# A hybrid decoder step with routed experts: dense stages and experts in one engine block, DRAM rows cleared later, exponentials of the gates ahead of the modulation copies

## The chip, the cores and the metric

One core of a Trainium2 chip runs the whole step. The metric is the device time of one execution in microseconds (us), as the median of several runs. All arithmetic is float32 but for a few small matmuls of zeros, ones and small integers in bfloat16.

## What is computed

One layer for 512 prompt tokens and 32 sample tokens (8 sequences of 4) with the same weights, width 1024:

```
mod = silu(c) @ w_ada + b_ada;  sh1, sc1, g1, sh2, sc2, g2 = split(mod)
h = rmsnorm(x, norm1) * (1 + sc1) + sh1
u, gate_b, gate_c, val = split(h @ w_in)               # 1024 x 2048
pool_out = (trailing means of u, windows 2/4/8/16, minus u) @ w_pool * pool_scale
conv_out = gate_b * depthwise_conv3(gate_c * val)
x = x + g1 * (concat(pool_out, conv_out) @ w_out)
h2 = rmsnorm(x, norm2) * (1 + sc2) + sh2
logits = h2 @ w_router + b_router;  top 4 of 32;  gates = softmax(of the four)
y = sum over the four experts: gate * (((u + 1) * g * sigmoid(1.702 g)) @ w_down[e] + b_down[e])
    with g = min(h2 @ w_gate[e] + b_gate[e], 7), u = clip(h2 @ w_up[e] + b_up[e], -7, 7)
x = x + g2 * y;  out = rmsnorm(x, final_norm)
```

The new states of the pooling and of the convolution (last 15 rows of u, last 2 rows of gate_c * val) are outputs too. The kernel evaluates all 32 experts, each on up to 96 rows: each expert has three matrices of 4 MB, 402 MB in all.

## The kernel before, in words

Tokens lie in 5 tiles: 4 of 128 prompt rows (PT = 4), one of the 32 sample rows (TT = 5 in all). Every engine has its own instruction stream; an operation waits for semaphores (`wait_ge`) and raises one (`then_inc`). The program has two parts, each an `nc.Block()` of its own: `block` (L335) for the dense stages and the router, `block2` (L1250) for the experts. Between them all five engines meet at a barrier (L1050), for the SBUF tensors of the first part are given back there (`part.close()`) and those of the second are laid over them. So that no DMA still reads or writes them, SyncE (SP) ends its first part with six waits (L375 to L380): for the stored rows of h2, for the stored states, for the cleared table and for the cleared rows.

**Weights.** SP issues all weight loads, 1 MB each. The dense stages take 36 of them through a ring of six slots (L343 to L346): a slot is loaded again when TensorE (PE) is done with what it held. The experts take 384 through twelve slots (`load`, L1256); the first twelve are fetched in the first part, `first` (L348), the last eight of them when the last dense slots come free. After that a pair of loads is issued for each pair of slots that `gate_up` frees (`mm_done`).

**Input projection** (`project`, L920). It has 16 column groups f of 128 columns. Group f is 32 matmuls over all 544 tokens into one of two PSUM tiles (`zt[f % 2]`), so PE may begin group f only when group f - 2 has been read out. For f = 0 to 3 (u) and f = 4 to 7 (gate_c) ScalarE (ACT) reads it out with `leave` (L566), two activations each, and raises `z_evac`; for f from 8 on VectorE (DVE) does. Groups 0 to 7 follow one another on PE without other work between them; after group 7 come the modulation matmuls of g1 (L855).

**ACT ahead of the first `leave`.** ACT issues DMAs: w_pool, w_router, b_router, norm2, 12 pieces of the expert biases (L558), and then, at L559 to L564, two that clear rows in DRAM from an SBUF tile of zeros: `expert_rows` (2176 rows of 4 KB, 8.9 MB) and `late_rows` (640 rows, 2.6 MB). Experts scatter their results into them from the third expert on; nothing before that needs them. An engine that issues a DMA goes on when the queue has taken it, not when it has landed.

**End of the first part.** For tile t: `mix` (w_out, 16 matmuls), the residual add, the norm, `transposes`, `router`; DVE's `best` picks the four experts; h2 rows go to DRAM (`store`, on SP for tiles 0 to 2, on ACT for 3 and 4). After the last tile PE computes each token's rank within its expert (L1043 to L1047) and raises `rank_done`.

**Start of the second part.** DVE: gates minus their maximum (L1595, raises `shifted`), `rank_m`, `members(0)`; PE turns members into row numbers (`row_ids`, L1758); DVE's `ids(0)` raises `id_ready`; GpSimd (POOL) gathers the rows of expert 0 with three indirect DMAs (L1310). DVE meanwhile works out the positions, waits for ACT's exponentials (`exp_done`, L1621), normalises the gates and then turns the gathered rows (`turn_rows(0)`, L1499), which is what PE's `gate_up(0)` (L1776) waits for. PE has spread the modulation g2 over rows before that: four matmuls into PSUM tile `tp` for the prompt, and, when ACT has copied them (L1414), four into the same `tp` for the samples, copied at L1416. ACT's exponentials (L1418) stand behind both copies.

POOL then gathers for expert 1 and scatters 20 slices of the table of slots; ACT loads the table, and from expert 2 on row numbers come from it. The order of the work within an engine is that in which the code is written.

## Time and profile before

| | us |
|---|---|
| median of 3 runs | 1371.39 |
| lowest and highest run | 1368.34, 1371.46 |
| the profiled execution, its own time | 1374.72 |
| its span in the trace | 1373.0 |

| engine | busy us | share of the span |
|---|---|---|
| PE matmuls | 1250.7 | 91% |
| PE weight loads | 593.1 | 43% |
| DVE | 476.9 | 35% |
| ACT | 131.0 | 10% |
| POOL | 256.1 | 19% |

The page has 493.34 MB moved by DMA, a mean of 359 GB/s over the span. The share of busy time is a mean over stages: PE is shown as busy through most of the span, but matmuls are pipelined and their ends are modelled. The dense stages end near 286 us; the barrier stands there; the experts' loop runs from about 306 to 1340 us; the rest is the final norm. Times below are from the span's start.

### The profile page before, as it was taken

The numbers are of one execution on the slowest core, as the hardware profiler recorded it, in microseconds if no ns is written. First come the engines' busy times: TensorE is split into PE (matmuls) and PEld (weight loads), VectorE is DVE, ScalarE is ACT, GpSimd is POOL, SyncE is SP. The second block draws the span as 40 slices with busy tenths as digits, with TensorE's granted clock in tenths as the row PEclk, the third lists the DMA queues.
The fourth block names the chain that finished last, engine by engine and source line by source line (L and its number), as shares of the span: only waits on it lengthen the run. The fifth ranks groups of instructions, "written<-read, shape, count | busy, mean of one in ns | idle before, by whom it ended". The sixth has DMA issues, their size and how long they took to land. (4 is left out here: it accounts for less than half of the span.)

```text
span 1373.0 us, 32053 instructions
## 1 busy us (share of the span) xinstructions
PE 1250.7 (91%) x13745; PEld 593.1 (43%) x13745; DVE 476.9 (35%) x698; ACT 131.0 (10%) x259; POOL 256.1 (19%) x317
## 2 busy tenths in 40 slices
PE   4599999859999999999999999999999999998670
PEld 2477764432444444444444444444444445444140
DVE  1031403354333344333333344333333333333366
ACT  3100001120000000010000000000000000000012
POOL 4001110016211111122211111122211111111111
PEclk9889999969999999999999999999999999999795
DMA  9965682167999999999999999999999999999944
GB/s 324 360 256 207 211 326 92 41 268 271 406 418 419 419 420 419 419 420 418 417 419 419 419 418 419 419 419 419 417 419 418 419 420 419 420 420 420 411 166 142
DMA packets 92931, 493.34 MB, mean 359 GB/s; under 512 B 15079, under 2 KB 25923, under 8 KB 43205
## 3 DMA queue, kind: packets, MB, share of 16 engines
q1 hardware_dynamic: 73650, 449.25, 80.5%
q0 software_dynamic: 12416, 20.89, 4.6%
q10 hardware_dynamic: 6835, 22.78, 4.3%
q8 instruction: 21, 0.34, 0.1%
q14 instruction: 9, 0.07, 0.0%
HBM read 470.64 MB, written 29.38 MB: 364 GB/s over the span
## 5 line engine op out<-in xcount | busy, mean ns | idle before, releaser
L1776 PE MATMUL acc<-raw_b,ht 128*32 128x512 f32 x3024 | 336.7, 600 | 12.9 <-DMA raw_b<-in_w_up 7.8
L1776 PE MATMUL acc<-raw,ht 128*32 128x512 f32 x2928 | 324.5, 599 | 10.0 <-DMA raw<-in_w_up 10.0
L1574 DVE TENSOR_TENSOR g_sb<-acc,bias_gu 128x768 f32<-128x768 f32 x32 | 30.6, 957 | 566.5 <-PE acc L1776 566.5
L1310 POOL DMA_INDIRECT rows<-h_rows,row_next x90 | 92.0, 1023 | 700.5 <-DVE row_next L1494 681.1
L1776 PEld LDWEIGHTS acc<-raw_b,ht 128*32 128x32 f32 x3024 | 103.8, 111 | 239.8 <-issue 233.9
L1776 PEld LDWEIGHTS acc<-raw,ht 128*32 128x32 f32 x2928 | 101.6, 111 | 214.4 <-issue 209.8
L1799 PE MATMUL acc<-raw_b,at 128*32 128x256 f32 x2976 | 166.5, 379 | 0.0
L1799 PE MATMUL acc<-raw,at 128*32 128x256 f32 x2976 | 166.5, 379 | 0.0
L938 PE MATMUL acc<-h_t,raw 128*128 128x288 f32 (+1 forms) x512 | 121.5, 400 | 15.6 <-ACT raw_b L571 14.4
L1799 PEld LDWEIGHTS acc<-raw_b,at 128*32 128x32 f32 x2976 | 102.9, 110 | 70.9 <-issue 18.0
L1799 PEld LDWEIGHTS acc<-raw,at 128*32 128x32 f32 x2976 | 102.9, 110 | 57.7
L938 PEld LDWEIGHTS acc<-h_t,raw 128*128 128x128 f32 x512 | 99.0, 194 | 38.0 <-issue 16.2
L1321 POOL DMA_INDIRECT expert_rows<-y_sb,y_idx x87 | 87.0, 1000 | 26.5 <-issue 26.5
L1397 ACT ACTIVATE a_sb<-g_sb 128x768 f32<-128x768 f32 x32 | 27.0, 844 | 618.7 <-DVE g_sb L1576 618.7
L1385 ACT ACTIVATE y_sb<-y_sb,table 128x256 f32<-128x256 f32 x96 | 41.8, 498 | 337.6 <-DVE y_sb L1516 337.6
L1508 DVE STREAM_TRANSPOSE at<-a_sb 128x768 f32<-128x768 f32 x31 | 49.7, 1602 | 64.9 <-PE acc L1799 64.9
L1499 DVE STREAM_TRANSPOSE ht<-rows 128x768 f32<-128x768 f32 x31 | 49.8, 1605 | 0.2
L855 PE MATMUL acc<-raw,c_act 128*32 128x256 f32 x384 | 25.1, 407 | 14.5 <-DMA raw<-in_w_ada 14.4
L1331 POOL DMA_INDIRECT late_rows<-y_sb,late_idx x9 | 16.9, 1881 | 81.7 <-ACT y_sb L1385 79.9
L1516 DVE TENSOR_TENSOR y_sb<-acc,bias_d 128x768 f32<-128x768 f32 x32 | 30.4, 950 | 4.4 <-DMA late_rows<-y_sb,late_idx 4.4
L982 PE MATMUL acc<-raw,raw_b 128*128 128x512 f32 x64 | 31.4, 647 | 0.0
L461 POOL DMA_DIRECT2D mod_rows<-mod x12 | 6.1, 506 | 134.3 <-DVE mod L654 125.2
(237 smaller groups left out, 651.1 us busy)
## 6 DMA issues: line engine op xcount, KB each, us to landing
raw<-in_w_down SPq DMA_DIRECT2D x66, 1024.0 KB, 20.8
raw_b<-in_w_gate SPq DMA_DIRECT2D x65, 1024.0 KB
raw_b<-in_w_up SPq DMA_DIRECT2D x65, 1024.0 KB, 13.6
raw<-in_w_gate SPq DMA_DIRECT2D x63, 1024.0 KB, 16.9
raw<-in_w_up SPq DMA_DIRECT2D x63, 1024.0 KB, 18.9
raw_b<-in_w_down SPq DMA_DIRECT2D x62, 1024.0 KB, 20.2
raw<-in_w_ada SPq DMA_DIRECT2D x24, 1024.0 KB, 12.0
expert_rows<-zeros ACTq DMA_DIRECT2D x1, 8704.0 KB, 30.6
```

What stands on the lines that cost most here:

```text
L938: mm = pe.matmul(zt[f % 2][:, b, 0:hi_ - lo_], w[:, j, (f % 2) * P:(f % 2 + 1) * P], h_t[:, j, lo_:hi_], start=(j == 0), stop=(j == KT - 1))
L982: mm = pe.matmul(out_[0:r, h, :], mix_t[j][:, t * P:t * P + r], w[:, j % KC, h * HALF:(h + 1) * HALF], start=(j == GR), stop=(j == GR - 1))
L1310: pool.indirect_dma_start(rows[:, b, :], None, h2_quarter, bass.IndirectOffsetOnAxis(ap=idx[:, b:b + 1], axis=0), bounds_check=Q * NTOK - ...
L1321: pool.indirect_dma_start(y_quarter, bass.IndirectOffsetOnAxis(ap=y_idx[:, b:b + 1], axis=0), y_sb[:, b, :], None, bounds_check=Q * ROWS - ...
L1385: act.activation(y_sb[:, b, :], y_sb[:, b, :], ACT.Copy, scale=gate).then_inc(y_scaled, 1)
L1397: act.activation(s_sb[:, :, :], g_sb[:, :, :], ACT.Sigmoid, scale=ALPHA).then_inc(sig_done, 1)
L1499: dve.transpose(ht_of(e)[:, :, :, :], turned(rows)).then_inc(ht_ready, 1)
L1508: dve.transpose(at_[:, :, :, :], turned(a_sb)).then_inc(at_ready, 1)
L1516: dve.tensor_tensor(y_sb[:, :, :], y, bias_d[:, :].unsqueeze(1).to_broadcast([P, SB, CW]), ALU.add)\
L1574: dve.tensor_tensor(g_sb[:, :, :], g_ps, plus(0), ALU.add).then_inc(g_read, 1)
L1776: mm = pe.matmul(gu_ps[b][q * TB:(q + 1) * TB, :].rearrange("p (m n) -> p m n", m=2), ht_of(i)[:, b, k, :], w[:, kk, :, q * CW:(q + 1) * C ...
L1799: mm = pe.matmul(out_[q * TB:(q + 1) * TB, b, :], x[:, b, k, :], w[:, kk, q * CW:(q + 1) * CW], start=(k == 0), stop=(k == KT - 1))
```

## The change

1. The two blocks become one. The barrier goes, and with it SP's six waits. In their place each engine's second part waits for what it needs itself: SP and POOL for `rank_done` and the stored h2 rows before anything else; DVE for `rank_done`, `rows_zeroed` and `table_blank` before its first write; POOL for `table_blank` before the table scatter and for `rows_zeroed` before its third step; ACT for the stored states before the second of its last fetches (`fetch(1)`, far later), whose tile `picked1` now lies where `gate_b` lay. `gate_b` and `picked1` are allocated first in their parts for that.
2. The two DMAs that clear rows are issued by ACT after the first four `leave` instead of before them.
3. ACT computes the exponentials first in its second part, and then copies g2.
4. The sample rows of g2 go to a PSUM bank of their own (`g2_s_ps`), in four pieces of 32 rows; so PE issues all eight spreading matmuls without waiting for a copy, and ACT copies once for the prompt and four times for the samples. `down(1)` waits for the copies, as its bank is the same.

```diff
-        block = part.enter_context(nc.Block())
+        block = top.enter_context(nc.Block())
...
-            sp.wait_ge(h2_stored[0], 16 * ((TT + 1) // 2))
-            sp.wait_ge(h2_stored[1], 16 * (TT // 2))
-            sp.wait_ge(state_stored, 16 * (2 + DEC_B))
-            sp.wait_ge(state_sent, 16 * (1 + DEC_T))
-            sp.wait_ge(table_blank, 16)
-            sp.wait_ge(rows_zeroed, 32)
...
+            for g in range(GR):
+                leave(g, uext[:, g, PAST:PAST + SEQ], uext_s[:, g, :, PAST:PAST + DEC_T])
+
             act.wait_ge(pool_step, POOL_STEPS)
             for dram in (y_dram, late_dram):
                 rows_ = dram.rearrange("(p r) n -> p r n", p=P)
                 act.dma_start(rows_, zeros[:, :].unsqueeze(1).to_broadcast([P, rows_.shape[1], D]))\
                     .then_inc(rows_zeroed, 16)
...
-            for g in range(GR):
-                leave(g, uext[:, g, PAST:PAST + SEQ], uext_s[:, g, :, PAST:PAST + DEC_T])
             for g in range(GR):
                 leave(GR + g, gate_c[:, g, 0:SEQ], by_seq(gate_c[:, g, SEQ:NTOK]))
...
+            g2_s_ps = psum[:, SB, 0:QW]
...
-            block2 = experts.enter_context(nc.Block())
-
-            @block2.sync
+            @block.sync
             def _(sp):
+
+                sp.wait_ge(rank_done, 1)
+                sp.wait_ge(h2_stored[0], 16 * ((TT + 1) // 2))
+                sp.wait_ge(h2_stored[1], 16 * (TT // 2))
                 sp.dma_start(fn_bc[:, :], final_norm.partition_broadcast(P)).then_inc(fn_loaded, 16)
...
-            @block2.gpsimd
+            @block.gpsimd
             def _(pool):
 
+                pool.wait_ge(rank_done, 1)
+                pool.wait_ge(h2_stored[0], 16 * ((TT + 1) // 2))
+                pool.wait_ge(h2_stored[1], 16 * (TT // 2))
                 pool.memset(rows[:, :, :], 0.0).then_inc(rows_filled, 1)
...
                 pool.wait_ge(entries_ready, 1)
+                pool.wait_ge(table_blank, 16)
...
                 step(1)
+                pool.wait_ge(rows_zeroed, 32)
                 step(2)
...
+                    if t == 1:
+                        act.wait_ge(state_stored, 16 * (2 + DEC_B))
+                        act.wait_ge(state_sent, 16 * (1 + DEC_T))
...
-                act.wait_ge(g2_spread, 1)
-                act.activation(g2_bc[:, :], flat(tp[:, :, :]), ACT.Copy).then_inc(g2_copied, 1)
-                act.wait_ge(g2_spread, 2)
-                act.activation(g2_bc_s[:, :], flat(tp[:, :, :])[0:NS, :], ACT.Copy).then_inc(g2_copied, 1)
                 act.wait_ge(shifted, 1)
                 act.activation(gates[:, :, :], gates[:, :, :], ACT.Exp).then_inc(exp_done, 1)
+                act.wait_ge(g2_spread, 2)
+                act.activation(g2_bc[:, :], flat(tp[:, :, :]), ACT.Copy).then_inc(g2_copied, 1)
+                for q in range(Q):
+                    act.activation(g2_bc_s[:, q * QW:(q + 1) * QW], g2_s_ps[q * NS:(q + 1) * NS, :], ACT.Copy)\
+                        .then_inc(g2_copied, 1)
...
+                dve.wait_ge(rank_done, 1)
+                dve.wait_ge(rows_zeroed, 32)
+                dve.wait_ge(table_blank, 16)
                 dve.tensor_tensor(gates[:, :, :], top_v[:, :, 0:TOPK], top_v[:, :, 0:1].to_broadcast([P, TT, TOPK]),
                                   ALU.subtract).then_inc(shifted, 1)
-                dve.wait_ge(rank_done, 1)
...
-                for n, (sel_, r) in enumerate(((sel_p, P), (sel_s, NS))):
-                    if n:
-                        pe.wait_ge(g2_copied, n)
-                    for q in range(Q):
-                        mm = pe.matmul(tp[0:r, q // 2, (q % 2) * QW:(q % 2 + 1) * QW], sel_[:, q, :],
-                                       mod_g2[:, :], start=True, stop=True)
-                    mm.then_inc(g2_spread, 1)
+                for q in range(Q):
+                    mm = pe.matmul(tp[:, q // 2, (q % 2) * QW:(q % 2 + 1) * QW], sel_p[:, q, :], mod_g2[:, :],
+                                   start=True, stop=True)
+                mm.then_inc(g2_spread, 1)
+                for q in range(Q):
+                    mm = pe.matmul(g2_s_ps[q * NS:(q + 1) * NS, :], sel_s[:, q, :], mod_g2[:, :], start=True, stop=True)
+                mm.then_inc(g2_spread, 1)
                 gate_up(0)
                 gate_up(1)
+                pe.wait_ge(g2_copied, 1 + Q)
                 down(1)
```

**ACT at the input projection.** The names are tiles and tensors, `raw_b` here the buffer that holds the rows of u, `gate_c` the gates of the convolution; in brackets the semaphores that an instruction waits for. Before:

```order
L558 DMA a_bc<-in_b_down 32x256 x4
L562 DMA expert_rows<-zeros 2176x1x1024 [waits pool_step]
L562 DMA late_rows<-zeros 640x1x1024
L569 ACTIVATE raw_b<-acc 128x512 [waits z_done]
L571 ACTIVATE raw_b<-acc 128x8x4
```

And now, the first group read out and the last of the four, and what follows:

```order
L553 DMA a_bc<-in_b_down 32x256 x4
L559 ACTIVATE raw_b<-acc 128x512 [waits z_done]
L561 ACTIVATE raw_b<-acc 128x8x4
...
L559 ACTIVATE raw_b<-acc 128x512 [waits z_done]
L561 ACTIVATE raw_b<-acc 128x8x4
L572 DMA expert_rows<-zeros 2176x1x1024 [waits pool_step]
L572 DMA late_rows<-zeros 640x1x1024
L559 ACTIVATE gate_c<-acc 128x512 [waits z_done]
```

The clearing moved behind the reading out of group 3 and ahead of that of group 4.

**ACT where the two parts meet.** `out<-gate_b` are the state stores. Before:

```order
L623 DMA out<-gate_b 16x512
L1050 UNCONDITIONAL_BRANCH
L1378 UNCONDITIONAL_BRANCH [waits barrier_Pool_Activation_PE_DVE_SP_release]
L1414 ACTIVATE g_bc<-acc 128x1024 [waits g2_spread]
L1416 ACTIVATE g_bc_s<-acc 32x1024 [waits g2_spread]
L1418 ACT_TABLE_LOAD
L1418 ACTIVATE gates<-gates 128x20 [waits shifted]
L1397 ACT_TABLE_LOAD
```

And now:

```order
L619 DMA out<-gate_b 16x512
L1384 UNCONDITIONAL_BRANCH
L1423 ACT_TABLE_LOAD
L1423 ACTIVATE gates<-gates 128x20 [waits shifted]
L1425 ACTIVATE g_bc<-acc 128x1024 [waits g2_spread]
L1427 ACTIVATE g_bc_s<-acc 32x256 x4
L1403 ACT_TABLE_LOAD
```

The barrier is gone, and the exponentials stand ahead of the copies.

**SP where the two parts meet.** Before:

```order
L351 DMA raw<-in_w_up 128x2048 [waits mix_done]
L1050 UNCONDITIONAL_BRANCH [waits state_sent,table_blank,state_stored,rows_zeroed,h2_stored1,h2_stored0]
L1252 UNCONDITIONAL_BRANCH [waits barrier_Pool_Activation_PE_DVE_SP_release]
L1254 DMA fn_bc<-in_final_norm 128x1024
L1260 DMA raw_b<-in_w_gate 128x2048 [waits mm_done]
```

And now:

```order
L352 DMA raw<-in_w_up 128x2048 [waits mix_done]
L1249 UNCONDITIONAL_BRANCH
L1255 DMA fn_bc<-in_final_norm 128x1024 [waits h2_stored1,h2_stored0,rank_done]
L1261 DMA raw_b<-in_w_gate 128x2048 [waits mm_done]
```

Of the six waits two are left, with `rank_done` beside them, and no other engine waits for SP there.

## Rows read from the trace of the kernel before

**Rows 1.** Busy us and counts of each engine in a stretch, granted clock, DMA share, GB/s.

```profile
400.00:1280.00 880.00, 871.46 (x10764) 371.94 (x10760) 302.89 (x397) 66.30 (x142) 175.19 (x171) 1.00 1.01 419
```

**Rows 2.** Timeline of PE, 41 to 118 us: start, duration, idle before in brackets.

```profile
41.45 14.92 PE L938 MATMUL acc<-h_t,raw 128*128 128x256 f32 x64 [1.15 <-DVE h_t L695]
70.80 47.20 PE L938 MATMUL acc<-h_t,raw 128*128 128x256 f32 x192 [14.43 <-ACT raw_b L571]
117.94 3.66 PE L855 MATMUL acc<-raw,c_act 128*32 128x256 f32 x64
```

**Rows 3.** Timeline of ACT, 53 to 89 us.

```profile
53.07 16.85 ACTq L562 DMA_DIRECT2D late_rows<-zeros  x1
69.97 0.60 ACT L569 ACTIVATE raw_b<-acc 128x512 f32<-128x512 f32 x1 [26.28 <-issue]
...
81.38 0.60 ACT L569 ACTIVATE raw_b<-acc 128x512 f32<-128x512 f32 x1 [10.14 <-PE acc L938]
...
88.71 0.60 ACT L569 ACTIVATE raw_b<-acc 128x512 f32<-128x512 f32 x1 [6.65 <-PE acc L938]
```

**Rows 4.** Stretches around the stall, columns as in the first group.

```profile
52.00:70.00 18.00, 4.37 (x19) 3.13 (x17) 0.00 (x0) 0.03 (x1) 0.00 (x0) 0.72 1.03 379
...
76.00:78.00 2.00, 2.00 (x8) 1.62 (x7) 0.00 (x0) 0.00 (x0) 0.00 (x0) 0.80 1.01 416
```

**Rows 5.** DMA issues by line: KB each, median us to landing.

```profile
late_rows<-zeros ACTq DMA_DIRECT2D x1, 2560.0 KB, 36.1
...
expert_rows<-y_sb,y_idx POOLq DMA_INDIRECT x87, 6.0
...
h_rows<-h_row ACTq DMA_DIRECT2D x1, 512.0 KB, 8.9
...
h_rows<-h_row ACTq DMA_DIRECT2D x1, 128.0 KB, 5.6
```

**Rows 6.** Waits of SP's queue at the barrier: total us, times, longest.

```profile
SPq L378 <- DMA out<-gate_b: 15.3, 1, 15.3
```

**Rows 7.** Timeline of POOL, 290 to 312 us.

```profile
290.99 0.74 POOL L1298 MEMSET rows<- 128x768 f32 x1 [21.18 <-POOLq L1050]
...
297.13 1.01 POOL L1310 DMA_INDIRECT rows<-h_rows,row_first  x1 [0.30 <-issue]
...
311.71 1.01 POOL L1310 DMA_INDIRECT rows<-h_rows,row_first  x1 [0.30 <-issue]
```

**Rows 8.** Timeline of ACT: the last store of h2.

```profile
280.60 0.31 ACTq L594 DMA_DIRECT2D h_rows<-h_row  x1
```

**Rows 9.** Timeline of DVE, 291 to 315 us.

```profile
291.03 0.18 DVE L1595 TENSOR_TENSOR gates<-top_v 128x20 f32<-128x20 f32 x1 [6.27 <-PEq L1050]
...
293.17 0.16 DVE L1488 TENSOR_TENSOR row_first<-acc,taken 128x3 uint32<-128x3 f32 x1
...
304.18 0.17 DVE L1622 TENSOR_REDUCE e_sum<-gates 128x5 f32<-128x20 f32 x1 [6.06 <-ACT gates L1418]
...
304.95 1.55 DVE L1499 STREAM_TRANSPOSE ht<-rows 128x768 f32<-128x768 f32 x1
...
314.47 1.64 DVE L1499 STREAM_TRANSPOSE y_sb<-rows 128x768 f32<-128x768 f32 x1 [6.15 <-DMA rows<-h_rows,row_first]
```

**Rows 10.** Timeline of PE, 285 to 325 us.

```profile
285.30 0.29 PE L1047 MATMUL acc<-mask_bf,ones_bf 128*128 128x32 bf16 x5
...
299.57 1.91 PE L1809 MATMUL acc<-mod_g,sel_s 128*32 128x256 f32 x8 [1.11 <-ACT g_bc L1414]
306.56 18.50 PE L1776 MATMUL acc<-raw_b,ht 128*32 128x512 f32 x144 [5.07 <-DVE ht L1499]
```

**Rows 11.** Timeline of SP's queue: the first slots that the experts' loop frees.

```profile
314.83 0.33 SPq L1260 DMA_DIRECT2D raw_b<-in_w_gate  x1
...
319.98 0.33 SPq L1260 DMA_DIRECT2D raw_b<-in_w_gate  x1
```

**Rows 12.** A stretch before and at the start of gate_up(0), columns as in the first group.

```profile
304.00:308.00 4.00, 1.44 (x8) 0.40 (x12) 3.50 (x9) 1.35 (x2) 0.00 (x0) 0.69 0.01 4
```

More of the change, by code:

```diff
@@ L137, in sb @@
             return part.enter_context(nc.sbuf_tensor(name, shape, dt))
+        gate_b = sb("gate_b", [P, GR, NTOK])
         mod = sb("mod", [P, PARTS * QW])
@@ L146, in hybrid_step @@
         h_t = sb("h_t", [P, KT, NTOK])
-        gate_b = sb("gate_b", [P, GR, NTOK])
         gate_c = sb("gate_c", [P, GR, NTOK])
@@ L558, in _ @@
                     act.dma_start(b_raw[q * E:(q + 1) * E, m, :], b[0, :, q * CW:(q + 1) * CW]).then_inc(bias_loaded, 16)
-            act.wait_ge(pool_step, POOL_STEPS)
-            for dram in (y_dram, late_dram):
-                rows_ = dram.rearrange("(p r) n -> p r n", p=P)
-                act.dma_start(rows_, zeros[:, :].unsqueeze(1).to_broadcast([P, rows_.shape[1], D]))\
-                    .then_inc(rows_zeroed, 16)
             def leave(f, dst, dst_s):
@@ L577, in _ @@
                 leave(g, uext[:, g, PAST:PAST + SEQ], uext_s[:, g, :, PAST:PAST + DEC_T])
+            act.wait_ge(pool_step, POOL_STEPS)
+            for dram in (y_dram, late_dram):
+                rows_ = dram.rearrange("(p r) n -> p r n", p=P)
+                act.dma_start(rows_, zeros[:, :].unsqueeze(1).to_broadcast([P, rows_.shape[1], D]))\
+                    .then_inc(rows_zeroed, 16)
             for g in range(GR):
@@ L1081, in sb @@
                 return experts.enter_context(nc.sbuf_tensor(name, shape, dt))
+            picked = [sb("picked1", [P, TOPK, D])]
             rows = sb("rows", [P, SB, CW])
@@ L1113, in hybrid_step @@
             fn_bc = sb("fn_bc", [P, D])
-            picked = [sb(f"picked{b}", [P, TOPK, D]) for b in range(2)]
+            picked.insert(0, sb("picked0", [P, TOPK, D]))
             made = picked[0][:, :, :].rearrange("p k d -> p (k d)")
@@ L1376, in _ @@
                 blocks(pool, body)
-            @block2.scalar
+            @block.scalar
             def _(act):
@@ L1464, in _ @@
                                    scale=1.0 / D).then_inc(fin_sqrt, 1)
-            @block2.vector
+            @block.vector
             def _(dve):
@@ L1747, in _ @@
                 finish(TT - 1)
-            @block2.tensor
+            @block.tensor
             def _(pe):
```

## The prediction

> **What bounds the kernel now.** I read the stretches first, then PE's timeline, then the two places where PE stands still.
>
> From 400 to 1280 us the DMA engines are full: share 1.01 at 419 GB/s [rows 1]. Every weight byte passes once, so the experts' loop cannot run faster than that; its end follows from when its loads begin. A load beyond the first twelve is issued when `gate_up(0)` has freed a pair of slots, first at 314.83 us and then every 5.15 us [rows 11]. A microsecond by which that first issue comes earlier is one off the end, for what follows (the loop, the last scatter, the final norm) is unchanged by the edit. So two things count: how early the dense part ends, and how long the seam between `rank_done` and `gate_up(0)` is.
>
> *Dense part.* PE runs groups 0 and 1 from 41.45 us for 14.92, then is idle for 14.43 us until 70.80, and the row names ACT's reading out of group 0 [rows 2]. ACT does it at 69.97 us; just before stands the issue of `late_rows<-zeros`, which held ACT's queue from 53.07 for 16.85 us [rows 3]. PE's wait is thus an issue stall of ACT. After it PE is slow for a while: group 2 takes 10.58 us (70.80 to 81.38), group 3 7.33 us (81.38 to 88.71) [rows 2, 3]. The granted clock was 0.5 after the idle time and 0.80 on average from 76 to 78 us [rows 4], so it was at the lower level (1.2 GHz) until about 77 us. From 118 us on PE sets the pace (idle times of a microsecond or two), and DMA is mostly not full.
>
> *Seam.* The last rank matmul ends at 285.59 us [rows 10], but DVE begins at 291.03 and POOL at 290.99, both behind the barrier [rows 7, 9]. It was SP that came last, and SP waited for the state stores, 15.3 us long [rows 6]. After that DVE is idle 6.06 us, until 304.18, for ACT's exponentials [rows 9], which stand behind two copies that wait for PE.
>
> **The change part by part.**
>
> *Clearing later, the old stall.* Without it group 2 begins when group 1 ends. ACT's last bias DMA was handed over before 53.07 us, so group 0 (done near 48.8) is read out by 54, ahead of the 56.37 at which group 2 may start. PE then needs 7.33 us for each of groups 2 to 7: 56.37 + 6 x 7.33 = 100.35, where it was 117.94 [rows 2]. That is **17.6 us**: 14.4 of waiting, 3.2 of the low clock. The weights are no limit: those for groups 2 to 7 were asked for by 41 us.
>
> *Clearing later, the new stall.* Group 3 ends at 71.03, ACT reads it out by 71.7, hands over the first DMA, and by 72.4 stands at the second, as it did at 53.07. How long it stands is not known, since its cause is not in a row. What is known: while it stood, the DMA engines moved 16.85 x 379 GB/s = 6.4 MB [rows 3, 4], of which about 1 MB was one weight chunk. If ACT is freed when as much of the zeros has gone, 5.3 MB, and one weight chunk (the slot freed by group 3) travels with it, then 6.4 MB at 419 GB/s take 15.2 us; part of the early traffic was the tail of small loads that will be gone, so I take 14.5. ACT is free at 86.9, group 4 read out at 87.6; PE wants that PSUM tile for group 6 at 56.37 + 4 x 7.33 = 85.69. New stall **1.9 us**, too short for the clock to fall. Bounds: none (gain 17.6); or the whole 16.85 us again, a stall of 4.3 us and then the clock loss of 3.2 (gain 10.1). Taken: gain **15.7 us**. The zeros themselves, 11.5 MB, are 27 us of full DMA from 72 us, done near 100. They run beside the loads for groups 8 on, wanted at 104 us and later, and that one chunk has 18 us for what takes 3 to 5. DVE's new wait for `rows_zeroed` is 170 us behind.
>
> The Trainium skill (DMA: Bandwidth & Descriptors, Issuing engines are not separate DMA queues) speaks against zeros beside weights: DMAs of all issuers end on the same 16 engines and interleave. By it the weight chunk's 2.5 us are part of ACT's hold, as counted above (15.7 gained); were the queues apart, the hold would be 12.0 us and the stall nothing (17.6 gained).
>
> *The barrier.* DVE's first instruction moves from 291.03 to about 285.7: 5.33 us. Its table of work is otherwise the same, so `row_first` is ready at 293.33 - 5.33 = 288.0 [rows 9]. POOL must have the h2 rows: issued at 280.60 [rows 8], landing 5.6 us later [rows 5], 286.2; its memset of 0.74 ends at 287, in time. The last of three gathers is issued at 297.13 - 5.33 = 291.8 [rows 7]. SP's state wait goes to ACT's `fetch(1)`, a thousand microseconds later: free.
>
> *The exponentials.* ACT ends its state stores at 285, loads its table and has the exponentials by about 287.5. DVE reaches them at 304.18 - 6.06 - 5.33 = 292.8 and does not wait. Three small operations, and at 293.4 it is ready to turn rows. Now the gather is late, not the exponentials. The eight loads of 1 MB issued from 271 on are still under way, and gathers must land among them. In quiet a gather took 314.47 - 311.71 = 2.76 us [rows 7, 9]; under full load rows of the same size scattered to DRAM landed in 6.0 us, and 512 KB of h2 in 8.9 [rows 5]. I take 6.0, the like operation at the like load: 297.8. So `turn_rows(0)` moves from 304.95 to 297.8, **7.1 us**; by the bounds 10.4 (294.56) and 4.2 (300.7). PE follows 1.61 us behind [rows 9, 10], at 299.4.
>
> *g2.* PE's eight spreading matmuls run on without the 1.11 us wait [rows 10]; nobody waits for them. They end near 295, so PE is idle 4.4 us before `gate_up(0)`. Before, it was idle from 301.48 to 306.56 and the clock fell at about 305.5 (mean 0.69 in 304 to 308 us [rows 12]), 4.0 us in. The first pair of slots then took 8.27 us (306.56 to 314.83) where the next took 5.15 [rows 10, 11]. With 4.4 us I take the fall as still happening: 0. If it does not, 3.1 us more. ACT has three more copies; it is idle then.
>
> *Sum.* 15.7 + 7.1 = 22.8 us. Profiled execution: 1374.72 - 22.8 = 1351.9. It is 3.3 us above the median of the runs, so for the median 1371.39 - 22.8 = **1348.6 us**.
>
> **The rivals.**
>
> A. *The stall moves whole.* ACT is held long enough, or by something else than the zeros' bytes, that PE loses at group 6 what it lost at group 2. For it: the cause of the 16.85 us is in no row. Against: PE has 14.7 us of groups 4 and 5 to run meanwhile, which it did not have before. Only the seam gains: 1371.4 - 7.1 = 1364.3.
>
> B. *The seam gives nothing*: the gather comes so late behind the loads that `gate_up(0)` keeps its distance from `rank_done`, or the merged block hides a wait of its own. Against: 5.33 + 6.06 us of plain waiting go. Only the dense part gains: 1355.7.
>
> C. *Slower.* ACT is held until `late_rows` has landed, 36.1 us after its issue [rows 5]: to 72.4 + 36.1 = 108.5, group 4 out at 109.2. PE then stalls 23.5 us at group 6 and 3.2 by the clock, 26.7 against 17.6 now: 9.1 lost. With the seam at its lower bound of 4.2 the kernel takes 1376.3. A hold of h costs h - 12.6 of stall and 3.2 of clock, h - 9.4 in all, against 17.6 and the seam's gain: it decides from 31.2 us (seam 4.2) or 34.1 us (seam 7.1) upward. Against it: ACT went on after 16.85 us before, far ahead of the landing. The Trainium skill (Perfetto Trace Analysis, DMA Instruction — HWDGE) has the descriptor generator freed once all descriptors are generated, which can be long before the landing; by it ACT would not wait for a landing, and C would fall away.
>
> D. *All bounds good*: no new stall, a quick gather, the clock kept: 17.6 + 10.4 + 3.1 = 31.1, so 1340.3.
>
> **How the numbers follow.** Forecast with its own bounds (gain 14.3 to 31.1, D as its end): 0.82. B 0.07, inside them. A 0.07. C 0.04. Range: 1340 to 1358, from D to the lower bounds (1357.1) and a little for the runs' own scatter; left out are A, C and what misses the bounds, not over 0.2. A measurement of this kernel can tell about 0.3%, 4.1 us, from no change. Faster than that: forecast, A and B, 0.96 less a remainder for what I have not seen, 0.94. C in its milder form is within 4.1 us of now: 0.03 the same, 0.03 slower.
>
> **What would show it.** Right: PE's L938 row of groups 2 to 7 begins right at 56 us, with a gap of 0 to 4 us near 86 whose releaser is ACT's reading into `gate_c`; ACT's `late_rows` issue is as long as before, now near 72; the g1 matmuls at 102 instead of 118. At the seam, DVE's first operation within 0.3 us of the last rank matmul, no idle time for ACT's exponentials, but 4 to 5 us for the DMA of the gathered rows; `gate_up(0)` 13.8 us after the rank matmuls (21.0 now). Each time from 400 us on the same rows, 419 GB/s. Wrong: an idle time of over 5 us on PE near 86, a weight DMA as its releaser anywhere before 180 us, or a loop that ends no earlier although it starts earlier.

## The result, and the profile after

| | before | after |
|---|---|---|
| median, us (lowest to highest, 4 runs each) | 1371.43 (1368.34 to 1373.71) | 1349.46 (1348.49 to 1350.94) |
| the profiled execution, its own time | 1374.72 | 1349.58 |
| its span | 1373.0 | 1347.7 |

The ratio is 0.984, with a 95% interval of 0.9818 to 0.9861: 22.0 us less by the medians, where 22.8 were forecast (1348.6 predicted, 1349.46 measured). Between the two profiled executions lie 25.1 us; 3.3 of them are the profiled run of before, which lies that much above its median.

From the page after: the span, the busy times of the engines and what DMA moved in all:

```profile
span 1347.7 us, 32046 instructions
PE 1244.0 (92%) x13745; PEld 593.0 (44%) x13745; DVE 477.9 (35%) x698; ACT 131.5 (10%) x262; POOL 256.3 (19%) x317
DMA packets 92931, 493.34 MB, mean 366 GB/s; under 512 B 15079, under 2 KB 25923, under 8 KB 43205
```

The bytes are those of before and so, within 1 us, are the busy times, but for PE's 6.7 us less; 3.2 of them are group 2, which no longer runs at the low clock after a stall. The rest of the gain is idle time. The middle of the experts' loop runs as in [rows 1], at 419 GB/s:

```profile
400.00:1280.00 880.00, 860.80 (x10564) 370.11 (x10556) 299.47 (x389) 64.47 (x138) 169.99 (x165) 0.99 1.02 419
```

**The input projection after.** PE's timeline, then ACT's (start, duration, in brackets the idle time before and what ended it). They answer to [rows 2] and [rows 3]:

```profile
42.24 44.25 PE L934 MATMUL acc<-h_t,raw 128*128 128x256 f32 x192 [1.15 <-DVE h_t L691]
87.22 14.90 PE L934 MATMUL acc<-h_t,raw 128*128 128x256 f32 x64 [0.73 <-ACT gate_c L561]
102.05 3.66 PE L851 MATMUL acc<-raw,c_act 128*32 128x256 f32 x64
```

```profile
71.86 0.65 ACTq L572 DMA_DIRECT2D expert_rows<-zeros  x1
72.55 13.79 ACTq L572 DMA_DIRECT2D late_rows<-zeros  x1
86.39 0.60 ACT L559 ACTIVATE gate_c<-acc 128x512 f32<-128x512 f32 x1 [13.84 <-issue]
```

PE now runs six groups on end, 192 matmuls, where it stood still for 14.43 us after two. The hold of ACT's queue has moved with the DMAs, from 53 to 72.55 us, and is shorter, 13.79 us. PE pays 0.73 us for it at group 6. The matmuls of g1 begin at 102.05 instead of 117.94.

**The seam after.** The last rank matmul and `gate_up(0)` on PE [rows 10]:

```profile
267.92 0.29 PE L1043 MATMUL acc<-mask_bf,ones_bf 128*128 128x32 bf16 x5
275.63 1.08 PE L1822 MATMUL acc<-mod_g,sel_s 128*32 128x256 f32 x8
```

DVE across it [rows 9]:

```profile
268.25 0.18 DVE L1608 TENSOR_TENSOR gates<-top_v 128x20 f32<-128x20 f32 x1 [0.86 <-PE acc L1043]
...
275.55 0.20 DVE L1636 TENSOR_TENSOR entry<-gates,e_sum 128x20 f32<-128x20 f32 x1
280.59 1.55 DVE L1509 STREAM_TRANSPOSE ht<-rows 128x768 f32<-128x768 f32 x1 [4.85 <-DMA rows<-h_rows,row_first]
```

POOL [rows 7], with the last of the three gathers, and ACT's exponentials:

```profile
268.84 0.74 POOL L1302 MEMSET rows<- 128x768 f32 x1 [16.23 <-DMA h_rows<-h_row]
...
274.36 1.01 POOL L1314 DMA_INDIRECT rows<-h_rows,row_first  x1 [0.30 <-issue]
```

```profile
267.59 1.28 ACT L1423 ACT_TABLE_LOAD   x1 [3.00 <-issue]
268.88 0.22 ACT L1423 ACTIVATE gates<-gates 128x20 f32<-128x20 f32 x1
```

DVE goes on 0.04 us after the last rank matmul (267.92 + 0.29 = 268.21) instead of 5.4 us. The exponentials are there at 269.10, long before DVE wants them. DVE is ready to turn rows at 275.75 and then waits 4.85 us for the gathered ones. PE begins `gate_up(0)` at 282.19, 13.98 us after the rank matmuls; it was 20.97. The first two pairs of slots come free, on SP's queue [rows 11], at:

```profile
289.91 0.33 SPq L1261 DMA_DIRECT2D raw_b<-in_w_gate  x1
...
295.06 0.33 SPq L1261 DMA_DIRECT2D raw_b<-in_w_gate  x1
```

That is 24.9 us earlier than 314.83, and the span is 25.3 us shorter. The gain made by 290 us is kept to the end, as the argument on the loop had it.

### The profile page after: what moved, and what is told of

The parts are those of the page before. It is cut to its first block and busy times, and to the rows that moved or that the text cites. A ratio compares the mean times of both kernels' runs of the same rounds, so it can differ in the third digit from the quotient of the medians.

```text
span 1347.7 us, 32046 instructions
## 1 busy us (share of the span) xinstructions
PE 1244.0 (92%) x13745; PEld 593.0 (44%) x13745; DVE 477.9 (35%) x698; ACT 131.5 (10%) x262; POOL 256.3 (19%) x317
## 2 busy tenths in 40 slices
DMA packets 92931, 493.34 MB, mean 366 GB/s; under 512 B 15079, under 2 KB 25923, under 8 KB 43205
## 5 line engine op out<-in xcount | busy, mean ns | idle before, releaser
L1788 PE MATMUL acc<-raw,ht 128*32 128x512 f32 x2928 | 323.8, 597 | 10.6 <-DMA raw<-in_w_up 10.6
L1811 PEld LDWEIGHTS acc<-raw_b,at 128*32 128x32 f32 x2976 | 104.1, 110 | 69.7 <-issue 17.9
L934 PE MATMUL acc<-h_t,raw 128*128 128x288 f32 (+1 forms) x512 | 118.5, 393 | 1.9 <-DVE h_t L691 1.1
L1596 DVE SCALAR_TENSOR_TENSOR a_sb<-u_sb,g_sb 128x768 f32<-128x768 f32 x32 | 30.7, 958 | 1.1
L1592 DVE TENSOR_TENSOR g_sb<-g_sb,a_sb 128x768 f32<-128x768 f32 x32 | 30.4, 951 | 0.0
## 6 DMA issues: line engine op xcount, KB each, us to landing
expert_rows<-zeros ACTq DMA_DIRECT2D x1, 8704.0 KB, 30.7
```

Of the source, the lines that this page charges most:

```text
L934: mm = pe.matmul(zt[f % 2][:, b, 0:hi_ - lo_], w[:, j, (f % 2) * P:(f % 2 + 1) * P], h_t[:, j, lo_:hi_], start=(j == 0), stop=(j == KT - 1))
L1592: dve.tensor_tensor(g_sb[:, :, :], g_sb[:, :, :], s_sb[:, :, :], ALU.mult).then_inc(glu_done, 1)
L1596: dve.scalar_tensor_tensor(out=a_sb[:, :, :], in0=u_sb[:, :, :], scalar=1.0, in1=g_sb[:, :, :], op0=ALU.add, op1=ALU.mult).then_inc(act_re ...
L1788: mm = pe.matmul(gu_ps[b][q * TB:(q + 1) * TB, :].rearrange("p (m n) -> p m n", m=2), ht_of(i)[:, b, k, :], w[:, kk, :, q * CW:(q + 1) * C ...
L1811: mm = pe.matmul(out_[q * TB:(q + 1) * TB, b, :], x[:, b, k, :], w[:, kk, q * CW:(q + 1) * CW], start=(k == 0), stop=(k == KT - 1))
```

## The experiments

Three sets of four, each set on one chip beside the kernel before. The first chip took 1370.95 us for the kernel before (median of 11), the second 1410.83 (of 9), the third 1404.18 (of 9). So each kernel is read against the kernel before of its own set; where kernels of different sets are compared, it is by these ratios or by stretches of their own traces. The result above is not recorded with a chip; its kernel before took 1371.43 us and its loop shows 419 GB/s, as on the first chip, so its traces stand below for that kind of chip. What makes the second and third chip slower became a question of its own.

### First set: the parts of the change one by one

**Clearing later alone.** The kernel before, with the two DMAs behind the first four `leave`:

```diff
-            act.wait_ge(pool_step, POOL_STEPS)
-            for dram in (y_dram, late_dram):
...
             for g in range(GR):
                 leave(g, uext[:, g, PAST:PAST + SEQ], uext_s[:, g, :, PAST:PAST + DEC_T])
+            act.wait_ge(pool_step, POOL_STEPS)
+            for dram in (y_dram, late_dram):
...
```

> Before, with only the clearing moved behind the first four readings of ACT; barrier, copies and exponentials as before. Theory (two independent gains: dense part 15.7 us, seam 7.1 us): 14.5 to 17.5 us faster than before, near 1356 us; PE's 14.4 us idle time at group 2 gone, under 2 us at group 6; the last rank matmul near 268 to 270 us; between it and gate_up(0) still 21 us, with DVE's 6 us wait for the exponentials. Rival (the stall moves whole to group 6): within 4 us of before, an idle time of over 10 us on PE near 86 us. Rival (the dense gain only shows once the barrier is gone, since DMA must catch up anyway): under 10 us faster.

Measured: 1355.84 us (1354.36 to 1360.06), ratio 0.9881 [0.9851, 0.9911]: 15.1 us less. PE's timeline:

```profile
42.78 46.94 PE L939 MATMUL acc<-h_t,raw 128*128 128x256 f32 x192 [1.15 <-DVE h_t L696]
90.50 14.90 PE L939 MATMUL acc<-h_t,raw 128*128 128x256 f32 x64 [0.78 <-ACT gate_c L566]
```

The long stall is gone and the new one is 0.78 us, without any other edit. The seam stays long: `gate_up(0)` begins 20.8 us after the last rank matmul.

**One block and exponentials first, clearing as before.**

```diff
@@ the kernel after @@
+            act.wait_ge(pool_step, POOL_STEPS)
+            for dram in (y_dram, late_dram):
...
             for g in range(GR):
                 leave(g, uext[:, g, PAST:PAST + SEQ], uext_s[:, g, :, PAST:PAST + DEC_T])
-            act.wait_ge(pool_step, POOL_STEPS)
-            for dram in (y_dram, late_dram):
...
```

> The changed kernel with the two clearing DMAs back ahead of ACT's first reading: barrier gone, exponentials first, g2 samples in their own bank. Theory: PE's 14.4 us stall at group 2 is back, and the seam (last rank matmul to gate_up(0)) is 14 us where it was 21; 6 to 8 us faster than before, near 1364.5 us. Rival (the seam's gain is eaten by the loads, which then collide with the gather): within 4 us of before.

Measured: 1363.93 us (1361.4 to 1369.31, 8 runs), ratio 0.9951 [0.9928, 0.9974]: 7.0 us less. `gate_up(0)` begins at 296.40, 14.3 us after the last rank matmul at 282.09. ACT and PE have the old stall back, 11.35 us of it instead of 14.43, since ACT was held 14.45 us and not 16.85 and the first two groups ran longer at a lower clock:

```profile
56.19 14.45 ACTq L557 DMA_DIRECT2D late_rows<-zeros  x1
```

```profile
71.52 38.69 PE L934 MATMUL acc<-h_t,raw 128*128 128x256 f32 x159 [11.35 <-ACT raw_b L566]
```

The two halves are worth 15.1 and 7.0 us alone; their sum is 22.1, and the whole change gave 22.0. The intervals of the halves are some 4 and 3 us wide to either side, so no interaction shows, and one of a few us is not excluded by the totals. The traces narrow it: the seam takes 14.3 us in this kernel and 14.0 in the change, and the new stall is 0.78 us without the merged block and 0.73 with it.

**Exponentials behind the copies again**, in the merged block (and g2 spread through the one tile `tp`):

```diff
+                act.wait_ge(g2_spread, 1)
+                act.activation(g2_bc[:, :], flat(tp[:, :, :]), ACT.Copy).then_inc(g2_copied, 1)
+                act.wait_ge(g2_spread, 2)
+                act.activation(g2_bc_s[:, :], flat(tp[:, :, :])[0:NS, :], ACT.Copy).then_inc(g2_copied, 1)
                 act.wait_ge(shifted, 1)
                 act.activation(gates[:, :, :], gates[:, :, :], ACT.Exp).then_inc(exp_done, 1)
```

> The changed kernel with the old order at g2: prompt matmuls, copy, sample matmuls into the same bank, copy, then the exponentials. Theory (the gathered rows are what DVE waits for now, they came 4.9 us after it was ready, so the exponentials have almost that much room): exponentials ready near 13.2 us after the last rank matmul, DVE turns the rows 1 to 2.5 us later than in the changed kernel, which then takes 1 to 2.5 us more, near 1351 us. Rival (the 6.06 us wait for the exponentials was the gain, the barrier hid nothing): 5 to 6 us more, near 1355 us.

Measured: 1353.93 us (1349.14 to 1356.78), ratio 0.9865 [0.9827, 0.9902]. The total can't tell this kernel from the change; the trace can. ACT, then DVE:

```profile
281.66 1.01 ACT L1425 ACTIVATE g_bc_s<-acc 32x1024 f32<-32x1024 f32 x1 [3.71 <-PE acc L1820]
282.70 1.28 ACT L1427 ACT_TABLE_LOAD   x1
283.99 0.22 ACT L1427 ACTIVATE gates<-gates 128x20 f32<-128x20 f32 x1
```

```profile
284.31 0.17 DVE L1633 TENSOR_REDUCE e_sum<-gates 128x5 f32<-128x20 f32 x1 [8.04 <-ACT gates L1427]
...
285.09 1.55 DVE L1508 STREAM_TRANSPOSE ht<-rows 128x768 f32<-128x768 f32 x1 [0.15 <-DVE entry L1635]
```

Rows are turned 15.7 us after the last rank matmul (269.41), against 12.4 in the change: in these two executions the edit is worth 3.3 us of the seam, where I had expected 1 to 2.5. The exponentials wait for both copies, and the second copy waits 3.71 us for PE's sample matmuls. These took 3.62 us here, at a granted clock of 0.50, and 1.91 us in the kernel before [rows 10], where the clock had risen. So 1.7 of the 3.3 us hang on the clock of this execution, and 1.6 are left without it, as expected. DVE waits 8.04 us for the exponentials here (6.06 before [rows 9]); with the exponentials first it waits 4.85 us for the gather instead.

**The small DMA first.** The order of the two DMAs is swapped, nothing else:

```diff
-            for dram in (y_dram, late_dram):
+            for dram in (late_dram, y_dram):
```

> The changed kernel with the two clearing DMAs in the other order: late_rows (640 rows of 4 KB) first, expert_rows (2176 rows) second. Theory G (the second DMA is held while the descriptors of the first are still being generated, and 640 fit at once): the second issue takes under 1.5 us instead of 13.8, ACT reads out group 4 in time, PE has no idle time at group 6; 0 to 1 us faster than the changed kernel. Rival L (an issue is held until enough bytes of all the zeros have gone, or its own descriptors are out): the second issue takes 10 us or more, PE stalls at group 6 as before or longer, the time is the same or up to 5 us more.

Measured: 1350.7 us (1348.78 to 1352.26), ratio 0.9845 [0.9815, 0.9876]. ACT and PE:

```profile
73.89 0.65 ACTq L572 DMA_DIRECT2D late_rows<-zeros  x1
74.57 0.66 ACTq L572 DMA_DIRECT2D expert_rows<-zeros  x1
```

```profile
42.00 61.17 PE L934 MATMUL acc<-h_t,raw 128*128 128x256 f32 x256 [1.15 <-DVE h_t L691]
```

With 2.6 MB ahead, neither issue is held: 0.65 and 0.66 us, and PE has no gap in eight groups. So the hold of 13.8 us is the second DMA's, while something of the 8.9 MB DMA ahead of it is still to be worked off. It is no landing: in the change `late_rows` was taken after 13.79 us, and `expert_rows` landed 30.7 us after its issue. The time is the change's within the scatter, as a gap of 0.73 us has to be.

### Second set: holding back loads, and clearing too late

The change still waits 4.85 us for a gather that lands beside eight weight loads. These kernels issue the last of those loads only when the gather has landed.

**Four loads held back.**

```diff
@@ SP, first part @@
-            for n in range(XSLOTS - OUT_CH, XSLOTS):
-                sp.wait_ge(*used(DENSE_CH - XSLOTS + n))
-                first(n)
@@ SP, second part, ahead of final_norm @@
+                sp.wait_ge(row_gathered, 16 * SB)
+                for n in range(XSLOTS - OUT_CH, XSLOTS):
+                    first(n)
```

> The changed kernel, but SP keeps back the last four of the twelve first expert loads (4 MB) until the rows of the first gather have landed. Theory (the gather is late because it travels among 8 MB of loads): the rows are turned 3 to 3.5 us earlier after the last rank matmul (12.4 us in the changed kernel, 9 here), the last gather landing 2.8 us after its issue instead of 6.2; but DMA is idle before it, and the 4 MB end near 19 us after the last rank matmul, so loads go on without a gap from there: 1.5 to 4 us faster than the changed kernel. Rival (a gather needs its 6 us whatever else is under way): the rows are turned as late as before, same time. Rival (the loads kept back are missed): slower than the changed kernel by 3 us or more, with a weight DMA as releaser of gate_up(0) or gate_up(1).

Measured: 1385.11 us (1377.89 to 1385.99), ratio 0.9799 [0.9767, 0.9831]. DVE's turn of the rows:

```profile
280.23 1.57 DVE L1512 STREAM_TRANSPOSE ht<-rows 128x768 f32<-128x768 f32 x1 [1.40 <-DMA rows<-h_rows,row_first]
```

It begins 8.9 us after the last rank matmul (271.30), 3.5 us sooner than in the change, and the wait is down from 4.85 to 1.40 us. So the gather was late for the loads beside it. What that is worth in total this set can't tell, since the change itself was not run in it; by the ratios the two overlap (0.984 [0.9818, 0.9861]).

**Two loads held back** (the same edit, with `XSLOTS - 2` in place of `XSLOTS - OUT_CH` for the loads that wait).

> The same with only the last two loads (2 MB) kept back. Theory: the other six are nearly through when the gathers are issued, so the rows are turned 2.5 to 3.5 us earlier than in the changed kernel, and the 2 MB are in before the first slots come free: 3 to 5 us faster than the changed kernel, so 1 to 2 us better than with four kept back. Rival (the sum of DMA work and idle time fixes the end, so order does not count): within 1.5 us of the changed kernel.

Measured: 1384.51 us (1381.48 to 1385.57, 5 runs), ratio 0.9808 [0.9786, 0.9829]; rows turned 8.9 us after the rank matmuls. Two are as good as four.

**Two loads held back and the small DMA first.**

> Two loads kept back, and late_rows cleared ahead of expert_rows. Theory: both gains add: no idle time of PE at group 6 (0.7 us) and the seam as with two kept back; 3 to 6 us faster than the changed kernel, near 1345 us. Rival (the runs' own scatter of 2 us hides it): not to be told from the run with two kept back, which is likely for 0.7 us.

Measured: 1382.7 us (1378.97 to 1384.02, 5 runs), ratio 0.9792 [0.9769, 0.9814]; rows turned 8.8 us after the rank matmuls, no gap at group 6. Against 0.984 for the change these ratios look a little better, but their intervals overlap and the chips differ. That was left to the third set.

**Clearing behind all eight `leave`.**

```diff
@@ the kernel after @@
+            for g in range(GR):
+                leave(GR + g, gate_c[:, g, 0:SEQ], by_seq(gate_c[:, g, SEQ:NTOK]))
             act.wait_ge(pool_step, POOL_STEPS)
             for dram in (y_dram, late_dram):
...
-            for g in range(GR):
-                leave(GR + g, gate_c[:, g, 0:SEQ], by_seq(gate_c[:, g, SEQ:NTOK]))
```

> The changed kernel with the two clearing DMAs behind all eight of ACT's readings, order as in the change. Theory: ACT is held 13 to 15 us again, but from 103 us, where it has nothing to do until 172 us; no idle time of PE near 86 us, 0 to 1 us faster than the changed kernel. Rival (the zeros, 27 us of DMA from 103 us, delay the weights of the projection's groups 10 on or of sh2): an idle time of PE with a weight DMA as releaser between 115 and 150 us, 2 us or more slower.

Measured: 1395.73 us (1394.33 to 1397.43), ratio 0.9887 [0.9863, 0.991], 11 to 13 us more than its three neighbours in the set. Those also hold loads back; against the change without that, 0.984 and 0.9815 in its own two sets, it is some 7 to 10 us. The rival of the expectation came true. ACT's issue and PE:

```profile
106.19 24.66 ACTq L574 DMA_DIRECT2D late_rows<-zeros  x1
```

```profile
151.20 9.20 PE L934 MATMUL acc<-h_t,raw 128*128 128x256 f32 x31 [9.03 <-DMA raw<-in_w_in]
```

PE waits 9.03 us for the chunk of w_in that group 12 uses, and the hold is 24.66 us instead of 13.8. SP issued that chunk at 123.95 us, while the zeros were under way (`late_rows` landed 55.1 us after its issue, at 161.3). In the change SP issued it at 120.61, and the zeros had landed by 110 (72.55 + 37.4). So the place behind four `leave` is not free by itself: there the zeros are gone before that chunk is asked for. The chunks that SP issued from 86.5 to 102.5 us in the change did travel beside the zeros, and PE waited for none of them.

### Third set: the same chip for the change, its successor and the question of the crawl

All four kernels of the second set lost time where the first set did not: after the first pair of slots, the second came free 26 to 29 us later instead of 5.15. PE's matmuls of `gate_up(0)` came a few at a time, with "issue" as the only releaser. I call this the crawl.

**The change again.**

> The change as it is, run beside the kernel with two loads held back. On a chip like the first: 1349 to 1352 us. On a chip like that of the second set (kernel before at 1411, 407 GB/s in the loop): theory (what those kernels lose at the start of the experts comes with the chip and not with the loads held back): 1385 to 1390 us, and here too the second pair of slots comes free 25 to 29 us after the first, with PE idle for 'issue' 14 to 20 us in gate_up(0). Rival (the loads held back cause it): the second pair comes 5.15 us after the first and the time is 1366 to 1372.

Measured: 1378.66 us (1375.31 to 1380.71, 5 runs), ratio 0.9815 [0.9794, 0.9835]. SP's queue:

```profile
293.38 0.33 SPq L1261 DMA_DIRECT2D raw_b<-in_w_gate  x1
...
307.85 0.33 SPq L1261 DMA_DIRECT2D raw_b<-in_w_gate  x1
...
321.50 0.81 SPq L1261 DMA_DIRECT2D raw_b<-in_w_down  x2
```

The second pair came 14.5 us after the first (less than the 25 to 29 I had written), the third 28.1 us after it; on the first chip these were 5.15 and 10.3. So held loads don't make the crawl: it is there without them, on a chip other than the first. The time is 6 us below the range I gave for a slow chip.

**The kernel before again.**

> The kernel before as it is, for its profile on this chip. Theory (the chip is what differed in the second set): on a chip like that one the steady stretch shows 406 to 408 GB/s instead of 419 and the second pair of slots comes 25 us or more after the first. On a chip like the first: rows as in the profile of the kernel before, the first pair at 313 to 317 us and the next 5.15 us later.

Measured: 1402.91 us (one run). The second pair came 20.7 us after the first (314.90, 335.57), the third at 343.14, 28.2 after; on the first chip 325.13 - 314.83 = 10.3. The crawl is there before the change too, and costs 28.2 - 10.3 = 17.9 us in this kernel and 28.1 - 10.3 = 17.8 in the change. It takes no part in the difference between them. The steady stretch showed 409 GB/s, a little above the 406 to 408 expected of a slow chip.

**Two loads held back and the small DMA first, again.**

> Theory: the two loads of gate and up weights held back leave the DMA engines to the gather, rows are turned 8.8 us after the last rank matmul where the change takes 12.4, and nothing later gives it back: 3 to 4 us less than the change on the same chip (ratio to the change 0.997 to 0.998). Rival: the loads come too late for the third matmul group pair or push the loads behind them, so that the time equals the change's within 1 us. On a chip like the first 1346 us by the theory, 1349 to 1350 by the rival.

Measured: 1371.19 us (1369.74 to 1372.21, 5 runs), ratio to the kernel before 0.9761 [0.9744, 0.9778]. The change took 1378.66 on this chip, and the two sets of runs don't overlap: **7.5 us less than the change** (1371.19 / 1378.66 = 0.995), where I had expected 3 to 4. The traces account for less: the two profiled executions lie 5.1 us apart (1377.30 and 1372.21), as follows. Rows are turned at 277.86, 8.8 us after the last rank matmul at 269.01; in the change on this chip at 284.51, 12.3 after 272.22. These 3.5 us are the held loads. `gate_up(0)` is then less idle ahead of it, and its first pair of slots takes 6.00 us (279.49 to 285.49) instead of 7.27: 1.3. The last rank matmul is 3.2 us earlier, of which 0.7 are the gap at group 6; the other 2.5 belong to no edit (a start 0.6 us sooner, and one group of w_out matmuls in 7.11 us that took 8.76 in the change). In all the first pair is freed 7.9 us earlier. The crawl takes 3.6 of them back: it lasts about as long as GpSimd's scatters do, and the third pair comes at 317.20, 5.5 us after their end, instead of 321.50, 3.1 us after it. So the edits' own share in this pair of traces is about 2 us behind the crawl, and 5.5 ahead of it; that they are faster on this chip is shown by the medians, and how much of the 7.5 us each of them gives is not.

PE in `gate_up(0)` of this kernel, its expert's first 144 matmuls:

```profile
279.49 10.66 PE L1794 MATMUL acc<-raw_b,ht 128*32 128x512 f32 x95 [0.19 <-DVE ht L1515]
290.53 4.90 PE L1794 MATMUL acc<-raw_b,ht 128*32 128x512 f32 x9 [0.38 <-issue]
296.25 0.59 PE L1794 MATMUL acc<-raw_b,ht 128*32 128x512 f32 x1 [0.81 <-issue]
297.65 5.11 PE L1794 MATMUL acc<-raw_b,ht 128*32 128x512 f32 x9 [0.82 <-issue]
...
312.51 4.22 PE L1794 MATMUL acc<-raw_b,ht 128*32 128x512 f32 x14 [1.50 <-issue]
```

POOL's 20 scatters into the table of slots run from 285.95 to 311.70 here, and from 292.58 to 318.36 in the change on this chip.

**The table filled by one scatter instead of 20.** This kernel leaves out 19 of the 20 slices of the table, so from the third expert on it gathers and scatters hardly any rows, and its output is not the layer's.

```diff
-                for t in range(TT):
+                for t in range(1):
                     r = norm_rows(t)
-                    for k in range(TOPK):
+                    for k in range(1):
                         pool.indirect_dma_start(table_dram, bass.IndirectOffsetOnAxis(ap=pos_i[0:r, t, k:k + 1], axis=0),
...
-                act.wait_ge(table_filled, 16 * TT * TOPK)
+                act.wait_ge(table_filled, 16)
```

> Leaves out 19 of the 20 scatters that fill the table of slots, so that experts from the third on gather and scatter almost no rows. In the second set PE ran at a crawl in gate_up(0) from 292 to 316 us in the kernel with two loads held back, which ends as GpSimd's last table scatter does. Theory (those scatters, 1.3 us apart, hold up PE's supply of instructions on that chip): on such a chip no idle time for 'issue' of over 2 us between the first and the second pair of slots, which come 5 us apart. Rival (the crawl has nothing to do with the scatters): still 25 us or more apart. On a chip like the first the pairs are 5.15 us apart in any case and nothing follows. The loop (weights alone) then shows at most 419 GB/s and ends within 10 us of the change's.

Measured: 1352.22 us, one run on the same chip as the three above. PE in `gate_up(0)`:

```profile
281.77 17.35 PE L1788 MATMUL acc<-raw_b,ht 128*32 128x512 f32 x144 [2.94 <-DVE ht L1509]
298.94 5.33 PE L1788 MATMUL acc<-raw,ht 128*32 128x512 f32 x48
```

The crawl is gone: 144 matmuls in 17.35 us, pairs of slots freed at 288.89, 294.03 and 299.18. So the crawl needs both, this kind of chip and the row of table scatters; on the first kind of chip the same scatters leave the pairs 5.15 us apart. That rests on one execution, but the second pair came 14.5 to 29 us after the first in all seven other profiles of the second and third chip. By which path the scatters reach PE's sequencer is open. The DMA engines were nearly idle meanwhile (2 GB/s from 300 to 308 us in the kernel with held loads). The Trainium skill (Runtime: NRT & Kernel Launch, Instruction fetch mechanics) has each sequencer fetch its instructions ahead through a DMA queue of its own, mostly hidden. No run here shows that the crawl is a late fetch, and the trace gives it little support. The profile's instruction queue moved the same 21 packets, 0.34 MB, in the change and in the kernel with one scatter. In the change on this chip one of these 16 KB packets starts at 287.23 us and the next at 315.43, each about 1 us long, so none is under way while PE's matmuls come in bursts of a few every 0.7 us.

From the third pair on, this kernel's last `late_rows` scatter is 1020.7 us away (299.18 to 1319.86), though 15 MB of rows are no longer moved (477.99 instead of 493.34 MB); in the change on the same chip it is 1023.1 (321.50 to 1344.61). The loop hardly gains from fewer bytes, so there PE and not DMA sets its pace. From 400 to 1280 us it moved 396 GB/s, the change 411, and the DMA engines are shown busy to a share of 0.99 and 1.01. A share near 1 thus does not say by itself that DMA is the limit.

## Why the prediction was right, point by point

*The old stall: right.* 17.6 us were forecast to go at groups 2 to 7, and PE's timeline has them on end; 16.6 went (without the new stall g1 would have begun at 101.3 instead of 117.94), since PE began the projection 0.8 us later than in the trace of before. The kernel with that edit alone gained 15.1 us, against 15.7 for the dense part.

*The new stall: right in place and sign, too large.* 1.9 us forecast, 0.73 measured. The term that was off is the hold of ACT: 14.5 taken, 13.79 measured. ACT reached the second DMA at 72.55, not 72.4, and PE, which began 0.8 us later, wanted the tile at 42.24 + 44.25 = 86.49 instead of 85.69. Together 1.9 - 0.7 + 0.15 - 0.8 = 0.55. The old stall's gain came out 1.0 too high and the new stall 1.2 too long, so the projection's 15.9 us against 15.7 forecast is in part two errors that cancel. The hold's length came near, its reason did not: from 72 to 86 us the engines moved 331 GB/s, so 13.79 us are 4.6 MB, not the 6.4 MB assumed, and ACT is not freed by a fixed number of bytes. What the hold is made of is better told by the swapped order: the second DMA waits for the large one ahead of it, not for a landing, and with the small one ahead it is not held. The reading beside the issuing queues (zeros and weights interleave) is borne out by the kernel that cleared behind eight `leave`: 24.66 us of hold and a wait of 9.03 us for weights. Rival A (the stall moves whole) and rival C (ACT held to the landing) are excluded by the 13.79 us.

*The barrier: right.* DVE begins 0.04 us after the rank matmuls; 5.4 before. POOL's memset ended at 269.58, 1.4 us after the rank matmuls, as forecast (287 against 285.6), and ahead of the row numbers.

*The exponentials and the gather: right.* DVE ready for the turn 7.5 us after the rank matmuls (275.75), 7.8 forecast (293.4 against 285.6); the gather landed about 6.2 us after its issue (274.36 to 280.59), 6.0 forecast; `gate_up(0)` 13.98 us after the rank matmuls, 13.8 forecast. The kernel with this half alone gained 7.0 us, 7.1 forecast (6.7 by the seam of its trace). Rival B (the seam gives nothing) falls with it, and so does D, which wanted no stall, a quick gather and the clock kept.

*g2 and the clock: right.* The clock still fell ahead of `gate_up(0)`. Stretches of 4 us (busy of each engine, granted clock, DMA share, GB/s), to be set beside [rows 12]:

```profile
278.00:282.00 4.00, 0.00 (x0) 0.00 (x0) 1.41 (x1) 2.47 (x5) 0.00 (x0) 0.75 0.76 300
282.00:286.00 4.00, 3.81 (x20) 0.99 (x24) 1.82 (x7) 0.00 (x0) 1.00 (x1) 0.50 0.02 7
286.00:290.00 4.00, 4.00 (x36) 1.04 (x32) 0.00 (x0) 0.00 (x0) 3.05 (x3) 0.89 0.29 89
```

PE had been idle 5.48 us, and the first pair took 7.72 us, 0.55 less than 8.27. Counted at nothing, it gave half a microsecond.

*What bounds the loop: a right consequence from a reason that is not the whole.* I had written that the DMA engines are full and the loop cannot run faster than that. The one-slice table shows that on the third chip its pace stays though bytes go, and PE waits there for no weights. On the first chip PE waits 19.2 us for weights in 880 (10.6 and 8.6 us ahead of its `gate_up` matmuls), so the two bounds lie within some 2% of each other there, as an estimate. Why the loop of the third chip is slower (411 GB/s in the change, PE without waits for weights) is not shown. Either way the loop starts earlier and takes as long, which is all that the sum used.

*What the sum left out.* The dense part of the profiled executions gained 17.4 us (rank matmuls at 268.21 instead of 285.59), the projection's 15.9 and about 1.5 more in the later dense stages. Two groups of w_out matmuls were slow before (8.40 and 8.81 us instead of 7.03), one after. That is the clock's scatter and not the edit. By the two traces the first pair of slots comes 24.9 us earlier (17.4 of the dense part, 7.0 of the seam, 0.5 of the first pair) and by the medians the kernel gains 22.0. The forecast of 22.8 lies between them; that it met the median within 1 us is luck, as the clock alone moves an execution by 2 to 3 us.

## What to carry to other kernels

A large DMA issued ahead of another on the same queue can cost its engine 14 to 25 us at the second issue: put it where that engine's next work is not wanted for as long and where the weights of the next steps are already there, and issue the small one first. At the seam between two stages, look at what each engine waits for in turn: the barrier, then the exponentials, then the gather each hid the next, and the loads fetched ahead were what made the gather late. Two of them held back until the rows had landed, with the small DMA first, beat the change by 7.5 us by the medians on the same chip, 5.1 by the profiled executions.

## What the runs showed of the hardware

*The clock at the start of the projection is a draw.* The granted clock from 42 to 46 us, in the kernel with one table scatter and in the change, on the same chip and with the same code up to the table of slots:

```profile
42.00:46.00 4.00, 4.00 (x19) 3.27 (x19) 2.01 (x7) 2.05 (x3) 0.00 (x0) 1.00 1.10 345
```

```profile
42.00:46.00 4.00, 3.18 (x8) 2.58 (x9) 2.90 (x8) 3.02 (x5) 0.00 (x0) 0.50 1.09 347
```

Once it is 1.00 (2.4 GHz) and once 0.50 (1.2 GHz). In both PE had been busy for 1.7 of the 2 us from 38 to 40 and less from 40 to 42 (0.63 and 1.15 us). The first six groups then take 44.25 us or 46.17, and groups 0 and 1 alone 14.92 us [rows 2] or, in the kernel with one block alone, 17.89. Of the 14 profiled executions four show the high level (both of the kernel before, the change, the one scatter) and ten the low one. It is a scatter of some 2 to 3 us that belongs to no edit, and the reason why the smaller edits were read from the seam's own rows.

*Chips differ in more than pace.* On the second and third chip the kernel before took 2.9% and 2.4% more. Of the 28 us between its profiled executions on the first and third chip, 18 are the crawl of one stretch, which the 20 small scatters bring out there and not on the first; some 10 are a slower loop (1027.3 us from the third pair to the last scatter, against 1017.5). A kernel's ratio carried over (0.984 and 0.9815 for the same change), its microseconds did not.
